# Gate and up products of the second-kind layers: each matmul over 512 tokens divided in two over 256 tokens

## What is computed

```
h = rmsnorm(x, g_ffn[l]) * (1.0 + sc2) + sh2
f = (jax.nn.silu(h @ ffn_w1[l]) * (h @ ffn_w3[l])) @ ffn_w2[l]
x = x + gt2 * f
```

## Time and profile before

| | |
|---|---|
| median of 3 runs | 3339.12 us (3335.82 to 3342.11) |
| the profiled execution's own time | 3335.76 us |
| its span in the trace | 3334.0 us |
| TensorE matmul busy (PE) | 3223.9 us, 97% of the span |
| TensorE weight load busy (PEld) | 2572.4 us, 77% |
| VectorE, ScalarE, GpSimd | 49%, 40%, 41% |
| matmuls of 512 tokens, `hHi` x `wHi` alone (L458) | 2992, mean record 396 ns |
| gate and up stage of the second kind, layer 0 | 2299.98 to 2542.63 us |
| the same, layer 1 | 2950.78 to 3193.43 us |

### The profile page before, as it was taken

How to read it: one execution, slowest core, us unless ns; L and a number is a source line. 1 busy time by engine, 2 the same in 40 slices (tenths; PEclk the granted TensorE clock), 3 DMA queues, 4 the chain that set the end, 5 groups by cost and what they waited for, 6 DMA issues and landing times. The chain is left out here.

```text
span 3334.0 us, 46255 instructions
## 1 busy us (share of the span) xinstructions
PE 3223.9 (97%) x16177; PEld 2572.4 (77%) x16177; DVE 1636.6 (49%) x2609; ACT 1347.1 (40%) x2110; POOL 1375.1 (41%) x694
## 2 busy tenths in 40 slices
PE   7999999999998999999999999999999989999998
PEld 5678887788886678887788886767888867778887
DVE  5843336655625843336665633863333238533332
ACT  5755555322225755555322224554222235532222
POOL 2233333444453233333444454534444435444444
PEclk8999999999999999999999999999999999999999
DMA  3122222255532122222255532202222222022232
GB/s 130 58 79 85 80 83 70 79 192 200 197 107 72 58 79 85 80 83 70 79 192 201 197 106 97 83 27 76 95 99 99 98 104 77 32 82 94 100 102 101
DMA packets 94334, 335.84 MB, mean 101 GB/s; under 512 B 11236, under 2 KB 12132, under 8 KB 93968
## 3 DMA queue, kind: packets, MB, share of 16 engines
q1 hardware_dynamic: 92640, 328.12, 28.6%
q10 hardware_dynamic: 1584, 6.29, 0.5%
HBM read 332.22 MB, written 8.44 MB: 102 GB/s over the span
## 5 line engine op out<-in xcount | busy, mean ns | idle before, releaser
L434 POOL TENSOR_TENSOR wLo<-wring,wHi 128x1024 fp32r<-128x1024 f32 x482 | 1173.3, 2434 | 1745.8 <-ACT wHi L414 1745.7
L458 PE MATMUL psG<-hHi,wHi 128*128 128x512 f32 x2992 | 1183.5, 396 | 12.3 <-ACT whole L1840 3.5
L458 PE MATMUL psG<-hLo,wHi 128*128 128x512 f32 x2992 | 1170.1, 391 | 11.0 <-POOL hLo L483 10.1
L458 PE MATMUL psG<-hHi,wLo 128*128 128x512 f32 x2992 | 1165.4, 390 | 0.0
L414 ACT ACTIVATE wHi<-wring 128x1024 fp32r<-128x1024 f32 x482 | 510.2, 1059 | 979.4 <-PE psG L458 950.3
L458 PEld LDWEIGHTS psG<-hHi,wHi 128*128 128x128 f32 x2992 | 562.2, 188 | 151.5 <-issue 25.7
L458 PEld LDWEIGHTS psG<-hLo,wHi 128*128 128x128 f32 x2992 | 561.8, 188 | 142.6 <-POOL hLo L483 24.9
L458 PEld LDWEIGHTS psG<-hHi,wLo 128*128 128x128 f32 x2992 | 562.5, 188 | 113.0 <-issue 0.5
L458 PE MATMUL psG<-hidHi,wHi 128*128 128x512 f32 x704 | 274.0, 389 | 1.0 <-DVE branch L1445 1.0
L458 PE MATMUL psG<-hidLo,wHi 128*128 128x512 f32 x704 | 273.9, 389 | 0.0
L458 PE MATMUL psG<-hidHi,wLo 128*128 128x512 f32 x704 | 273.9, 389 | 0.0
(11 more groups left out here) (323 smaller groups left out, 3461.8 us busy)
## 6 DMA issues: line engine op xcount, KB each, us to landing
wring<-in_w SPq DMA_DIRECT2D x494, 512.0 KB, 3.3
modw<-in_wmod SPq DMA_DIRECT2D x96, 512.0 KB, 5.3
e_copies<-e_rows ACTq DMA_DIRECT2D x8, 512.0 KB
T_tab<-e_copies SPq DMA_DIRECT2D x4, 1024.0 KB, 5.5
mask<-in_mask SPq DMA_DIRECT2D x2, 1536.0 KB, 6.2
xin_sb<-in_x SPq DMA_DIRECT2D x4, 512.0 KB, 5.3
e_copies<-e_rows ACTq DMA_DIRECT2D x8, 256.0 KB
out<-o_sb SPq DMA_DIRECT2D x4, 512.0 KB, 3.8
```

The lines of the kernel that those rows point to most:

```text
L434: pool.tensor_tensor(wLo[:, c % CUTS, :, :], wring[:, c % RING, :, :], wHi[:, c % CUTS, :, :], ALU.subtract).then_inc(w_cut[c % CUTS], 1)
L458: mm = pe.matmul(psG[:, G.slot(u), :], w[:, c % CUTS, k, :], r(j), start=start and j == 0 and n == 0, stop=stop and j == len(kts) - 1 and ...
```

## The change

`gemm` gets a list of column ranges, `cols`. By default it is one range of all 512 tokens, and nothing changes. The gate and up products of the second kind pass two ranges, tokens 0 to 255 and 256 to 511. Each matmul becomes two, with the same block of weights as stationary operand, the same PSUM slot, and each half its own tokens. The start flag stands on the first matmul of a tile alone, the stop flag and the semaphore on the last.

```diff
-        def gemm(pe, u, c, rhs, kts, i=None, Ku=0, Kc=0, start=True, stop=True, ready=None, used=True):
+        def gemm(pe, u, c, rhs, kts, i=None, Ku=0, Kc=0, start=True, stop=True, ready=None, used=True,
+                 cols=(slice(0, SEQ),)):
...
-                    mm = pe.matmul(psG[:, G.slot(u), :], w[:, c % CUTS, k, :], r(j),
-                                   start=start and j == 0 and n == 0, stop=stop and j == len(kts) - 1 and n == 2)
+                    for at in cols:
+                        mm = pe.matmul(psG[:, G.slot(u), at], w[:, c % CUTS, k, :], r(j)[:, at],
+                                       start=start and j == 0 and n == 0 and at is cols[0],
+                                       stop=stop and j == len(kts) - 1 and n == 2 and at is cols[-1])
...
-                            gemm(pe, g_GU2 + j, CH2_GU + j, h, all_k, i, 4, 4, ready=None if j else h_done(1))
+                            gemm(pe, g_GU2 + j, CH2_GU + j, h, all_k, i, 4, 4, ready=None if j else h_done(1),
+                                 cols=(slice(0, SEQ // 2), slice(SEQ // 2, SEQ)))
```

## The result

The changed kernel takes 3363.57 us (median of 4 runs, 3362.63 to 3368.2) against 3337.47 us before (median of 4, 3334.67 to 3342.11): ratio 1.0081, 95% interval 1.0068 to 1.0095. That is +26.1 us by the medians, +27 by the ratio, where +28.1 was forecast.

A forecast was written before the change was run, and what follows sets the result against it. The prediction took TensorE's distance between matmul starts as the bound: 2112 x (240.0 - 226.7) ns = +28.1 us, and 3339.1 + 28.1 gives 3367 us. The range, to hold 8 in 10, was 3336 to 3398 us.

The forecast's parts named there:

- TensorE's pace bounds the stages: Gate and up stages of the second kind: they last as long as TensorE's matmul starts take, 226.7 ns each before.
- 13.3 ns belong to the matmul, not to its columns: Gate and up matmuls: each half pays the full 13.3 ns beside streaming, 120.0 ns a half, +28.1 us; chance 0.56.
- two open readings: The 13.3 ns in gate and up: per matmul (pair 240.0 ns, 0.56) or growing with columns (pair 226.7, rival B, 0.22).
- A floor of 112 ns from the load: Gate and up halves: weight loads follow each other at 112 ns, 224 a pair, with 107 ns of streaming hidden under it.
- rival C: Gate and up halves: load and streaming hinder each other; if floor and fixed cost add, pair 251 ns, +51 us; chance 0.16.
- rival D: Gate and up halves: 256 fp32r columns stream as float32 does, pair 436 ns, +442 us, 3781 us; chance 0.04.
- Issue and the longer loop cost nothing: Gate and up loop: starting twice the instructions, and a body of 192 matmuls instead of 96, adds no time.
- The size: Both gate and up stages of the second kind: 2112 added matmuls x 13.3 ns = +28.1 us, 14 in each layer.
- the head's waits: First chunk of each stage waits for low words; at most 0.6 us of added time hides there, left out.

The follow-up runs named there:

- the order of halves: Divided kernel, but in three of four chunks of a turn all matmuls of tokens 0 to 255 come first, then all of 256 to 511: 3364.69 us.

## Why the prediction was right

- *TensorE's pace bounds the stages, and what it loses goes to the end.* Right: 27.6 us in the stages, 28.5 in the span, no new wait, the rest of the program unmoved.
- *13.3 ns belong to the matmul, not to its columns.* Right, and chosen between two open readings with 0.56 against 0.22: 120.0 ns for 256 columns, 146.5 for 320, 173.2 for 384. That it is paid for each matmul, whatever its weights or its place in PSUM, is shown by the order of halves. The reason given for it, though, was partly wrong: "changing the weights is done as often as there are matmuls" suggests the loads, and half a load costs no less. Packed bfloat16 pays 2.4 to 2.9 ns, and most of the rest comes with the moving operand, probably with its columns being four bytes apart. Why a cost of that kind is paid once a matmul, and not by the column, stays open. So the size was right by the choice of reading, not by knowing the cause.
- *A floor of 112 ns from the load, 107 ns of streaming under it.* Right where equal matmuls follow each other, though read from float32 rows: 112 ns at 192 and at 128 columns. Where long and short alternate, the pair takes 2 ns less than by this rule and single starts are 0.09 us apart, so it is no least distance between matmuls. 120 is just above it. At 192 and 320 columns the one added matmul of a pair costs 256.6 - 226.7 = 30 ns, not 13.3.
- *Streaming and load side by side* (rival C, 0.16). It did not happen: PEld is busy for the whole window and the pace is 120.0.
- *Loss of the fast rate* (rival D, 0.04). Out: 120.0 ns at 256 columns, 112 at 192. It was also priced too low. The rows of float32 stand for records, and a float32 matmul is two of them here, each with a load of its own: L1768 issues 8 matmuls where the timeline has x16, L872 two where it has x4, L536 eleven where it has x22. So a float32 matmul of 256 columns takes 2 x 218 = 436 ns, four array cycles a column and not two, and the rival would have been some 870 ns a pair. The 112 and 218 ns hold for a record, which is how the sum used them. The reading of L536 is weaker than it was told, as the 22 loads are two for each of 11 matmuls; that each half has a load is shown by the 2112 more loads of the changed kernel.
- *Issue and the longer loop cost nothing.* Right: no step in the stage stands out, and 528 matmuls in a loop don't either.
- *The size.* 27.6 us in the stages against 28.1: the 0.3 us a layer that hide in the head's waits, named and left out, are the rest: the first chunk should have grown by 24 x 13.3 ns = 0.32 us and grew by 0.04.

## What to carry to other kernels

Where TensorE runs without gaps at 2.4 GHz, an fp32r matmul of 256 to 512 columns costs its columns / 2.4 plus 13.3 ns, and in a row of equal ones with full loads 112 ns is the least that was seen: so fewer and longer matmuls, and 512 columns where the tile allows it. Read the price off the distance between starts in a window; PE's busy share was 97% before and after. If matmuls are made shorter for another reason, keep them above some 240 columns (an estimate: where the two figures meet). And before an order of matmuls is changed inside a chunk, look at what the first chunk of a stage waits for: work that stood between the waits was what kept TensorE busy.

## What the runs showed of the hardware that was not expected

- What a bfloat16 matmul reads as moving operand matters: 512 packed columns of a constant tile take 216.2 ns, the same number four bytes apart in the activations 225.0.
- A bfloat16 load behind an fp32r matmul is not made ahead (0.27 us of idle before it), and a change there and back costs 20 to 30 ns.
- A float32 matmul is two records, each of them with a load and two array cycles a column; an fp32r or bfloat16 matmul is one.
- With 192 and 320 columns in turn, matmuls start 0.09 and 0.17 us apart; the loads start 0.11 and 0.15 apart.
- A stationary block of 64 columns makes the matmul no faster, but 3 ns slower (230 for 226.7).
- At a granted clock of 0.5 (the 1.2 GHz level) 384 fp32r columns take 0.32 us, their bare streaming: the 13.3 ns were seen at 2.4 GHz alone.
